# A two-block sequence kernel: the values' weighing in the forward state sweep, on VectorE or on GpSimd

## The chip, the cores and the metric

The kernel runs on one core of a Trainium2 chip. The metric is the device time of one execution in microseconds (us), as the median of several executions. The engines are named as in the profile: PE is TensorE's matmul, PEld its weight load, DVE is VectorE, ACT is ScalarE, POOL is GpSimd, SP is SyncE, which here only issues DMAs.

## The reference, cut to what matters

Two network blocks follow each other on 1024 tokens of width 1024 in float32. The second one has a bidirectional state-space mixer with 16 heads of 64 values, 2 groups and a state of 128. It works in chunks of 128 tokens. For one direction:

```python
xdt = (xs * dt[..., None]).reshape(b, nc, CHUNK, g, r, p)
acs = jnp.cumsum((dt * a).reshape(b, nc, CHUNK, g, r), axis=2)
decay = jnp.exp(jnp.where(lower, acs[:, :, :, None] - acs[:, :, None, :], -jnp.inf))
cb = jnp.einsum('bctgn,bcsgn->bctsg', cc, bc)
y_diag = jnp.einsum('bctsgr,bcsgrp->bctgrp', cb[..., None] * decay, xdt)
st = jnp.einsum('bcsgn,bcsgr,bcsgrp->bcgrpn', bc, jnp.exp(acs[:, :, -1:] - acs), xdt)
def step(s, inp):            # one chunk after the other
    dec, add = inp
    return s * dec[..., None, None] + add, s
y_off = jnp.einsum('bctgn,bcgrpn,bctgr->bctgrp', cc, s_in, jnp.exp(acs))
```

The product `st` takes the values (xs) of a chunk multiplied by one weight per token and head, dt * exp(acs_last - acs). This multiplication is the weighing that the change is about. It gives 128 tokens x 1024 values.

## The kernel before, in words

Everything but the scan is matrix products, for which a stream of 512 KB weight tiles is loaded by SP into `w_raw`. Each tile is split by GpSimd into a high and a low part, a cast at L195 and a subtraction at L197 (`stream_split`), and multiplied by TensorE at L204, L206 and L208. The scan of the second block is `phase5`, a block of its own: all engines meet at its end before the next phase (`phase6`) starts, whose first work is to load the rows that the scan left in memory (L2737 to L2739).

`phase5` has two halves. In the backward sweep (loop at L2642) the chunks are walked from the last to the first while TensorE also works on the stream's last sixteen tiles before the pool weights. GpSimd splits those and, last, the two tiles of the pool weights; it has no instruction in the forward half. The order of each engine's work is the order of its code; semaphores tie the engines together.

The forward sweep walks the eight chunks (i = 0 to 7). Each engine runs its own loop:

- VectorE (L2674): `add_decays(i)`, two sums of exponentials (L2664); `last_sum(i - 1)`, which ends the output rows of the chunk before (L2669, waits for TensorE's diagonal product) and, for the first five chunks, also makes the low part of a pooled tile (L2672, waits for ScalarE's high part L2579); two products of the decays with `cb` (L2681, `w_ready`, one for each group); the off-diagonal rows out of PSUM (L2688) and their addition (L2691); the state's update, times the decay (L2694) and plus the product in PSUM (L2695, `state_ready`); and the weighing of the next chunk's values into `xw` (`weigh(i + 1, 0)`, which is L2594, `xw_ready`). The weighing of chunk 0 stands ahead of the loop (L2659).
- TensorE (`forward`, L2469): the off-diagonal product (L2473, waits for `state_ready`); the state's product from `xw` (L2479, waits for `xw_ready` and for `y_ready`, which `last_sum(i - 1)` gives, and signals `st_done`); four exponent products of the next chunk (L2456, L2459, each waits for the exponential two before it); `cb` of the next chunk (L2465); the 16 diagonal products (L2489).
- ScalarE (L2571): four exponentials for the next chunk (L2558; the first two wait also for the `w_ready` of group 0 of the current chunk, the last two for that of group 1); a copy of `cb` (L2566); 16 copies that make the moving rows of the chunk after that (L2522); for i below 5 the high part (L2579).
- SP loads the backward sweep's output rows and the pooled tiles (L2394, L2398).

`xw` is one buffer. Its reader is the state's product L2479. L2594 is also the line of the weighings in the backward sweep and for the context, since they share the helper `weigh`.

Of the kernel before, what the change touches and what calls it, by code (L numbers as in the profile page):

```python
# [16 lines left out]
NC = SEQ // P  # L17
# [112 lines left out]
def bc(ap, dim, n):  # L130

    ap = ap.unsqueeze(dim)
    shape = list(ap.shape)
    shape[dim] = n
    return ap.broadcast_to(shape)
# [52 lines left out]
def stream_split(pool, k, first, last):  # L188

    for n in range(first, last):  # L190
        s = n % 2
        pool.wait_ge(k.w_loaded[s], (n // 2 + 1) * 16)
        if n >= 2:
            pool.wait_ge(k.tile_done, n - 1)
        pool.tensor_copy(k.w_hi[:, s, :], k.w_raw[:, s, :]).then_inc(k.w_high, 1)  # L195
        pool.wait_ge(k.w_high, n + 1)
        pool.tensor_tensor(k.w_lo[:, s, :], k.w_raw[:, s, :], k.w_hi[:, s, :].bitcast(F32),  # L197
                           ALU.subtract).then_inc(k.w_split, 1)
# [820 lines left out]
def signals(nc, ctx, stage, names):  # L1019

    return {n: ctx.enter_context(nc.semaphore(f"{stage}_{n}")) for n in names.split()}
# [1300 lines left out]
def phase5(nc, k, d, v):  # L2322
# [4 lines left out]
    with ExitStack() as ctx:  # L2327
        def sb(n, shape, dt=F32):
            return ctx.enter_context(nc.sbuf_tensor(n, shape, dt))

        def over(n, tile):
# [3 lines left out]
        state, y_even, xw = (sb(n, [P, SEQ]) for n in ("state5", "y5", "xw5"))  # L2335
# [21 lines left out]
        s = signals(nc, ctx, "p5", "chain xw_ready moving_ready d_done e_ready e_sum w_ready cb_done cb_ready off_done fore_ready fore_added "  # L2357
                                   "st_done state_ready diag_done y_ready y_back y_out0 y_out1 y_in0 y_in1 z_out d_out "
                                   "d_in dhi dlo x_done x_free0 x_free1 cleared area_in pooled")
# [10 lines left out]
        fwd = back + BWD_JOBS * NC  # L2370
        block = ctx.enter_context(nc.Block())

        def heads(ap):
            return ap.rearrange("p (h n) -> p h n", h=SSM_HEADS)

        def values(c):
            return heads(v.tok[:, c, VAL:VAL + D_MODEL])

        def per_head(buf, c, r, n=HDIM):

            return bc(buf[:, c, SSM_HEADS * r:SSM_HEADS * (r + 1)], 2, n)

        @block.sync
        def _(sp):
            stream_load(sp, k, XBC_END + 4, UZ_END + 4)
            sp.wait_ge(s["z_out"], 16 * KT)
            for i in range(NC):
                if i < 2:
                    sp.wait_ge(s["y_back"], 16 * NC)
                else:  # L2390
                    sp.wait_ge(y_out[i % 2], 16 * (i // 2))
                if i == 1:
                    sp.wait_ge(k.tile_done, UZ_END)
                sp.dma_start(y_of[i % 2], d.y_tok[i, :, :]).then_inc(y_in[i % 2], 16)  # L2394
                if i < SPLIT_EARLY:
                    sp.wait_ge(s["d_out"], 16 * KT)
                    sp.wait_ge(s["dlo"], i)
                    sp.dma_start(stage[:, :], d.u_scr[i, :, :]).then_inc(s["d_in"], 16)  # L2398

        @block.gpsimd  # L2400
        def _(pool):
            pool.memset(big[:, 0:2, :], 0.0).then_inc(s["cleared"], 1)
            pool.memset(pad[:, :], 0.0).then_inc(s["cleared"], 1)
            stream_split(pool, k, XBC_END + 2, UZ_END + 2)

        @block.tensor
        def _(pe):
# [180 lines left out]
        def _(dve):  # L2588
# [3 lines left out]
            def weigh(c, r, out=xw[:, :]):  # L2592

                tt(heads(out), values(c), per_head(v.w_st, c, r), ALU.mult).then_inc(s["xw_ready"], 1)  # L2594
# [61 lines left out]
            dve.wait_ge(s["pooled"], KT)  # L2656
            dve.wait_ge(x_free[1], fwd // 2)
            dve.tensor_copy(state[:, :].rearrange("p (a n) -> p a n", a=4), state_f).then_inc(s["state_ready"], 1)
            weigh(0, 0)  # L2659

            def add_decays(i):
                for g in range(NGRP):
                    dve.wait_ge(s["e_ready"], EXPS * i + 2 * g + 2)
                    tt(big[:, 2 * g, :], big[:, 2 * g, :], big[:, 2 * g + 1, :], ALU.add).then_inc(s["e_sum"], 1)  # L2664

            def last_sum(i):
                dve.wait_ge(s["diag_done"], i + 1)
                dve.wait_ge(s["fore_added"], i + 1)
                tt(y_of[i % 2], y_of[i % 2], Xf[(i + 1) % 2], ALU.add).then_inc(s["y_ready"], 1)  # L2669
                if i < SPLIT_EARLY:  # L2670
                    dve.wait_ge(s["dhi"], i + 1)
                    tt(v.a_lo[:, i, :], stage[:, :], v.a_hi[:, i, :].bitcast(F32), ALU.subtract).then_inc(s["dlo"], 1)  # L2672

            for i in range(NC):  # L2674
                add_decays(i)
                if i:
                    last_sum(i - 1)
                dve.wait_ge(s["cb_ready"], i + 1)
                for g in range(NGRP):
                    dve.wait_ge(s["e_sum"], 2 * i + g + 1)  # L2680
                    tt(weights[g].rearrange("p (h t) -> p h t", h=HPG), big[:, 2 * g, :].rearrange("p (h t) -> p h t", h=HPG),  # L2681
                       bc(cb[:, g, :], 1, HPG), ALU.mult).then_inc(s["w_ready"], 1)
                dve.wait_ge(s["off_done"], i + 1)
                if i:
                    dve.wait_ge(s["y_ready"], NC + i)
                else:
                    dve.wait_ge(s["d_out"], 16 * KT)
                tt(heads(fore_tmp), heads(Xf[(i + 1) % 2]), per_head(v.e_acs, i, 0), ALU.mult).then_inc(s["fore_ready"], 1)  # L2688
                dve.wait_ge(y_in[i % 2], 16 * (i // 2 + 1))
                dve.wait_ge(s["fore_ready"], i + 1)  # L2690
                tt(y_of[i % 2], y_of[i % 2], fore_tmp, ALU.add).then_inc(s["fore_added"], 1)  # L2691
                dve.wait_ge(s["st_done"], i + 1)
                dve.wait_ge(s["state_ready"], i + 1)
                ch.link(tt(heads(state[:, :]), heads(state[:, :]), per_head(v.e_tot, i, 0), ALU.mult))  # L2694
                tt(state[:, :], state[:, :], Xf[i % 2], ALU.add).then_inc(s["state_ready"], 1)  # L2695
                if i + 1 < NC:
                    weigh(i + 1, 0)
            last_sum(NC - 1)


# [241 lines left out]
def build(nc, arrays, out):  # L2942
# [14 lines left out]
    with ExitStack() as ctx:  # L2957
        k = open_kit(nc, ctx, d)
        phase1(nc, k, d)
        with ExitStack() as half:  # L2960
            w = open_work(nc, half, "b1", k)
            turn1 = Turn(nc, half, "n1", k, w, lambda t: k.vecs[:, VEC["mix_post"][0] + t:VEC["mix_post"][0] + t + 1],
                         (lambda t: k.vecs[:, VEC["mlp_pre"][0] + t:VEC["mlp_pre"][0] + t + 1], None), loads=True)
            turn2 = Turn(nc, half, "n2", k, w, lambda t: k.vecs[:, VEC["mlp_post"][0] + t:VEC["mlp_post"][0] + t + 1],
                         (lambda t: k.mod[:, MOD_AX, t:t + 1], lambda t: k.mod[:, MOD_BX, t:t + 1]))
            one_block(nc, phase2(nc, half, k, d, w, turn1),
                      mlp_phase(nc, half, k, d, w, P1_TILES + P2_TILES, "m1", turn1, turn2, ada=True,
                                out=d.x2_scr, ahead=True))
        with ExitStack() as half:
            clear_semaphores(nc)  # L2970
            v = open_scan(nc, half, k)
            phase4(nc, k, d, v)
            phase5(nc, k, d, v)
        with ExitStack() as half:
            clear_semaphores(nc)
            w = open_work(nc, half, "b2", k)
            turn3 = Turn(nc, half, "n3", k, w, lambda t: k.mod[:, MOD_G1, t:t + 1],
                         (lambda t: k.mod[:, MOD_A2, t:t + 1], lambda t: k.mod[:, MOD_B2, t:t + 1]), loads=True)
            turn4 = Turn(nc, half, "n4", k, w, lambda t: k.mod[:, MOD_G2, t:t + 1])
            one_block(nc, phase6(nc, half, k, d, w, turn3),  # L2980
                      mlp_phase(nc, half, k, d, w, OUT2_END, "m2", turn3, turn4, out=out))
# [146 lines left out]
```

## Time and profile before

| what | us |
|---|---|
| median of 3 runs | 2850.29 (2841.47 to 2863.74) |
| the profiled execution, its own time | 2847.84 |
| its span, first to last instruction | 2846.1 |
| PE busy | 2690.4 (95%) |
| DVE busy | 1659.4 (58%) |
| POOL busy | 987.9 (35%) |
| ACT busy | 607.8 (21%) |

The span is what the trace's clock covers; 1.74 us of the profiled execution's own time lie around it. All start times are counted from the span's start. In the timelines a row is one instruction, or several alike in a row (x2), with start, duration, engine, line, output <- inputs, and in brackets how long the engine had been idle and what ended that. PE is busy nearly throughout over the whole program, but shares of a whole program say little of one stage: the forward sweep is the stretch from 1740 to 1852 us.

### The profile page before, as it was taken

The numbers are of one execution on the slowest core, as the hardware profiler recorded it, in microseconds if no ns is written. First come the engines' busy times: TensorE is split into PE (matmuls) and PEld (weight loads), VectorE is DVE, ScalarE is ACT, GpSimd is POOL, SyncE is SP. The second block draws the span as 40 slices with busy tenths as digits, with TensorE's granted clock in tenths as the row PEclk, the third lists the DMA queues.
The fourth block names the chain that finished last, engine by engine and source line by source line (L and its number), as shares of the span: only waits on it lengthen the run. The fifth ranks groups of instructions, "written<-read, shape, count | busy, mean of one in ns | idle before, by whom it ended". The sixth has DMA issues, their size and how long they took to land. (4 is left out here: it accounts for less than half of the span.)

```text
span 2846.1 us, 32173 instructions
## 1 busy us (share of the span) xinstructions
PE 2690.4 (95%) x12390; PEld 2144.4 (75%) x12390; DVE 1659.4 (58%) x2219; ACT 607.8 (21%) x871; POOL 987.9 (35%) x515
## 2 busy tenths in 40 slices
PE   8889999999999999987898999989999999999997
PEld 5777877778888888766775776578767888888885
DVE  7887545756555665676747986953475222222247
ACT  4323232310110001133331104632131110001111
POOL 2212226553433333541212331023645333333353
PEclk9999999999999999998999999999999999999998
DMA  3111132223222232231001333241332111111122
GB/s 139 38 53 49 44 140 89 89 82 111 89 87 92 93 103 94 91 108 53 30 29 41 115 119 115 100 172 43 118 97 83 51 44 52 44 52 44 52 68 103
DMA packets 88484, 228.88 MB, mean 80 GB/s; under 512 B 27520, under 2 KB 30720, under 8 KB 88384
## 3 DMA queue, kind: packets, MB, share of 16 engines
q1 hardware_dynamic: 52384, 172.81, 18.5%
q10 hardware_dynamic: 36000, 54.69, 6.2%
q8 instruction: 68, 1.11, 0.2%
q14 instruction: 32, 0.26, 0.0%
HBM read 197.98 MB, written 28.31 MB: 80 GB/s over the span
## 5 line engine op out<-in xcount | busy, mean ns | idle before, releaser
L195 POOL CAST w_hi<-w_raw 128x1024 fp32r<-128x1024 f32 x254 | 288.3, 1135 | 1793.4 <-PE ps L208 1775.9
L204 PE MATMUL ps<-a_hi,w_hi 128*128 128x512 f32 x2080 | 693.3, 401 | 46.6 <-PEq L2931 14.6
L197 POOL TENSOR_TENSOR w_lo<-w_raw,w_hi 128x1024 fp32r<-128x1024 f32 x254 | 696.6, 2743 | 20.4
L206 PE MATMUL ps<-a_lo,w_hi 128*128 128x512 f32 x2080 | 677.8, 393 | 0.0
L208 PE MATMUL ps<-a_hi,w_lo 128*128 128x512 f32 x2080 | 675.2, 392 | 0.0
L204 PEld LDWEIGHTS ps<-a_hi,w_hi 128*128 128x128 f32 x2080 | 390.2, 190 | 148.9 <-issue 57.6
L206 PEld LDWEIGHTS ps<-a_lo,w_hi 128*128 128x128 f32 x2080 | 395.7, 190 | 83.4
L208 PEld LDWEIGHTS ps<-a_hi,w_lo 128*128 128x128 f32 x2080 | 394.7, 190 | 84.6
L206 PE MATMUL ps<-g_b,w_hi 128*128 128x512 f32 x1216 | 421.1, 397 | 0.0
L204 PE MATMUL ps<-g_b,w_hi 128*128 128x512 f32 x1088 | 369.4, 396 | 10.3 <-DVE g_b L1792 10.3
L208 PE MATMUL ps<-g_b,w_lo 128*128 128x512 f32 x1088 | 370.0, 397 | 0.0
L206 PEld LDWEIGHTS ps<-g_b,w_hi 128*128 128x128 f32 x1216 | 229.6, 189 | 53.4
L204 PEld LDWEIGHTS ps<-g_b,w_hi 128*128 128x128 f32 x1088 | 204.9, 188 | 67.6 <-DVE g_b L1792 14.2
L208 PEld LDWEIGHTS ps<-g_b,w_lo 128*128 128x128 f32 x1088 | 205.0, 188 | 49.9
L1750 ACT ACTIVATE tmp_b<-ps 128x1024 f32<-128x1024 f32 x48 | 49.3, 1027 | 863.6 <-PE ps L208 863.6
L1872 DVE TENSOR_TENSOR tmp_b<-tmp_b 128x1024 f32<-128x1024 f32 x48 | 58.8, 1225 | 299.1 <-ACT tmp_b L1750 299.1
L1885 DVE TENSOR_TENSOR mix_b<-mix_b,ps 128x1024 f32<-128x1024 f32 x48 | 58.6, 1220 | 250.6 <-PE ps L208 250.6
L1874 DVE TENSOR_TENSOR g_b<-tmp_b,g_b 128x1024 fp32r<-128x1024 f32 x48 | 106.6, 2220 | 54.1 <-ACT g_b L1754 54.1
L1144 DVE TENSOR_TENSOR acc_b<-acc_b,tmp_b 128x512 f32<-128x512 f32 x56 | 77.2, 1378 | 23.9 <-ACT tmp_b L1103 20.6
L2258 DVE SCALAR_TENSOR_TENSOR cv<-raw,vecs,cv 128x1284 f32<-128x1284 f32 (+1 forms) x48 | 80.4, 1676 | 5.3 <-DVE cv L2256 0.6
L1864 DVE SCALAR_TENSOR_TENSOR ada_sum_m<-ada_w,c_silu,ada_sum_m 128x128 f32<-128x128 f32 x252 | 74.7, 346 | 3.0
L1864 DVE SCALAR_TENSOR_TENSOR ada_sum_m<-ada_w_m,c_silu,ada_sum_m 128x128 f32<-128x128 f32 x252 | 74.6, 344 | 3.0
(459 smaller groups left out, 2680.6 us busy)
## 6 DMA issues: line engine op xcount, KB each, us to landing
w_raw<-in_wstream SPq DMA_DIRECT2D x254, 512.0 KB, 3.4
ada_w<-in_ada_w ACTq DMA_DIRECT2D x25, 512.0 KB, 3.5
ada_w_m<-in_ada_w ACTq DMA_DIRECT2D x25, 512.0 KB, 3.4
y_by_token<-y ACTq DMA_DIRECT2D x12, 512.0 KB, 3.3
x_res_b<-in_xT SPq DMA_DIRECT2D x2, 2048.0 KB, 11.5
x_block<-x_res_b SPq DMA_DIRECT2D x16, 256.0 KB, 3.1
z_rows<-ada_w ACTq DMA_DIRECT2D x8, 512.0 KB, 2.9
u_rows<-pad ACTq DMA_DIRECT2D x8, 512.0 KB, 4.2
```

The source lines that it names most:

```text
L195: pool.tensor_copy(k.w_hi[:, s, :], k.w_raw[:, s, :]).then_inc(k.w_high, 1)
L197: pool.tensor_tensor(k.w_lo[:, s, :], k.w_raw[:, s, :], k.w_hi[:, s, :].bitcast(F32), ALU.subtract).then_inc(k.w_split, 1)
L204: pe.matmul(o, w_hi, a_hi[:, c], start=first, stop=False)
L206: pe.matmul(o, w_hi, a_lo[:, c], start=False, stop=False)
L208: ins = pe.matmul(o, w_lo, a_hi[:, c], start=False, stop=last)
L1144: dve.tensor_tensor(w.acc[:, cols], w.acc[:, cols], w.tmp[:, t % 2, cols], ALU.add).then_inc(self.added, 1)
L1750: act.activation(w.tmp[:, t % 2, :], pair[t % 2], ACT.Relu).then_inc(k.pair_free[t % 2], 1)
L1864: ins = dve.scalar_tensor_tensor(out=sums, in0=weights, scalar=k.c_silu[:, kt, c:c + 1], in1=sums, op0=ALU.mult, op1=ALU.add)
L1872: tt(w.tmp[:, t % 2, :], w.tmp[:, t % 2, :], w.tmp[:, t % 2, :], ALU.mult).then_inc(s["square"], 1)
L1874: tt(w.g_lo[:, t, :], w.tmp[:, t % 2, :], w.g_hi[:, t, :].bitcast(F32), ALU.subtract)\
L1885: tt(w.mix[:, 2 * t, :], w.mix[:, 2 * t, :], pair[q], ALU.add).then_inc(k.pair_free[q], 1)
L2258: ins = stt(out=out, in0=raw[:, m:m + cols], scalar=tap(m), in1=out, op0=ALU.mult, op1=ALU.add)
```

## The change

GpSimd, once it has split its last tile, makes the weighed values of all eight chunks. The weighing of chunk 0 waits for the last product of the backward sweep, that of chunk i for the state's product of chunk i - 1, because both use the one `xw`. VectorE no longer weighs in the forward sweep. Nothing else changes, and `xw_ready` counts as before.

```diff
@@ gpsimd of phase5 @@
             stream_split(pool, k, XBC_END + 2, UZ_END + 2)
+            pool.wait_ge(s["x_done"], fwd)
+            for i in range(NC):
+                if i:
+                    pool.wait_ge(s["st_done"], i)
+                pool.tensor_tensor(heads(xw[:, :]), values(i), per_head(v.w_st, i, 0), ALU.mult).then_inc(s["xw_ready"], 1)
@@ vector of phase5 @@
             dve.tensor_copy(state[:, :].rearrange("p (a n) -> p a n", a=4), state_f).then_inc(s["state_ready"], 1)
-            weigh(0, 0)
@@ the loop's end @@
                 tt(state[:, :], state[:, :], Xf[i % 2], ALU.add).then_inc(s["state_ready"], 1)
-                if i + 1 < NC:
-                    weigh(i + 1, 0)
             last_sum(NC - 1)
```

## Rows read from the trace of the kernel before

**Rows 1.** Busy time in two stretches of the sweep.

```profile
core 0: us, PE busy (x) PEld busy (x) DVE busy (x) ACT busy (x) POOL busy (x), PEclk, DMA share, GB/s
1740.00:1756.00 16.00, 13.41 (x40) 6.03 (x40) 9.96 (x9) 12.86 (x25) 2.97 (x2) 1.00 0.50 171
1756.00:1830.00 74.00, 71.44 (x344) 44.50 (x344) 66.50 (x58) 55.94 (x127) 0.00 (x0) 1.00 0.28 100
```

**Rows 2.** The chain that ended last, just after the sweep: start, length.

```profile
1860.01 26.97 DMA mix_b<-z_rows
```

**Rows 3.** Timeline of VectorE in the forward sweep: an early period, and starts of later ones.

```profile
1761.65 1.22 DVE L2669 TENSOR_TENSOR y<-y,ps 128x1024 f32<-128x1024 f32 x1 [1.88 <-PE ps L2489]
1764.43 1.22 DVE L2672 TENSOR_TENSOR a_lo<-ada_w,a_hi 128x1024 fp32r<-128x1024 f32 x1 [1.55 <-ACT a_hi L2579]
1765.57 2.35 DVE L2681 TENSOR_TENSOR tok<-big,pad 128x1024 f32<-128x1024 f32 x2
...
1772.70 1.22 DVE L2594 TENSOR_TENSOR xw<-tok,w_st 128x1024 f32<-128x1024 f32 x1
1773.83 2.35 DVE L2664 TENSOR_TENSOR big<-big 128x1024 f32<-128x1024 f32 x2
1776.10 1.22 DVE L2669 TENSOR_TENSOR y_odd<-y_odd,ps 128x1024 f32<-128x1024 f32 x1
1777.65 1.22 DVE L2672 TENSOR_TENSOR a_lo<-ada_w,a_hi 128x1024 fp32r<-128x1024 f32 x1 [0.33 <-ACT a_hi L2579]
...
1818.56 1.23 DVE L2672 TENSOR_TENSOR a_lo<-ada_w,a_hi 128x1024 fp32r<-128x1024 f32 x1 [0.94 <-ACT a_hi L2579]
...
1830.23 1.21 DVE L2669 TENSOR_TENSOR y_odd<-y_odd,ps 128x1024 f32<-128x1024 f32 x1
...
1842.86 1.22 DVE L2669 TENSOR_TENSOR y<-y,ps 128x1024 f32<-128x1024 f32 x1 [0.88 <-PE ps L2489]
```

**Rows 4.** Timeline of ScalarE: the first exponential of three chunks.

```profile
1766.88 1.94 ACT L2558 ACTIVATE big<-ps 128x1024 f32<-128x1024 f32 x2 [2.49 <-DVE tok L2681]
...
1780.59 1.03 ACT L2558 ACTIVATE big<-ps 128x1024 f32<-128x1024 f32 x1 [2.97 <-PE ps L2459]
...
1834.71 1.03 ACT L2558 ACTIVATE big<-ps 128x1024 f32<-128x1024 f32 x1 [3.88 <-PE ps L2459]
```

**Rows 5.** Timeline of TensorE: a tile's last product, and the state's product twice.

```profile
1738.81 0.61 PE L208 MATMUL ps<-a_hi,w_lo 128*128 128x512 f32 x2
...
1748.23 1.88 PE L2479 MATMUL ps<-xw,tok 128*128 128x512 f32 x4
...
1763.23 1.88 PE L2479 MATMUL ps<-xw,tok 128*128 128x512 f32 x4
```

**Rows 6.** Timeline, GpSimd in the backward sweep, and its last split.

```profile
1655.16 3.38 POOL L197 TENSOR_TENSOR w_lo<-w_raw,w_hi 128x1024 fp32r<-128x1024 f32 x1
1663.91 1.69 POOL L195 CAST w_hi<-w_raw 128x1024 fp32r<-128x1024 f32 x1 [5.37 <-PE ps L208]
1665.67 3.24 POOL L197 TENSOR_TENSOR w_lo<-w_raw,w_hi 128x1024 fp32r<-128x1024 f32 x1
...
1739.57 1.04 POOL L195 CAST w_hi<-w_raw 128x1024 fp32r<-128x1024 f32 x1 [6.44 <-PE ps L208]
1740.68 2.37 POOL L197 TENSOR_TENSOR w_lo<-w_raw,w_hi 128x1024 fp32r<-128x1024 f32 x1
```

**Rows 7.** Timeline of VectorE beside those splits.

```profile
1654.10 2.19 DVE L2624 TENSOR_TENSOR tok<-big 128x1152 f32<-128x1152 f32 x1
1656.33 3.30 DVE L2624 TENSOR_TENSOR pad<-tok 128x1024 f32<-128x1024 f32 x1
...
1663.47 1.22 DVE L2631 TENSOR_TENSOR pad<-pad,big 128x1024 f32<-128x1024 f32 x1
1664.62 2.06 DVE L2645 TENSOR_TENSOR y<-tok,head_rows 128x1024 f32<-128x1024 f32 x1
1666.71 1.22 DVE L2647 TENSOR_TENSOR big<-ps,e_acs 128x1024 f32<-128x1024 f32 x1
```

## The prediction

> **What bounds the kernel now.** First I read the page: PE is busy for 95% of the span, so a stage counts only where PE waits in it. Then the busy time by stretch [rows 1]: from 1756 to 1830 VectorE is busy 66.50 of 74 us and PE 71.44, but PE's number holds waits between short groups of matmuls, and GpSimd does nothing at all. So the forward sweep is a loop over several engines, which has to be read from the timelines. Third, the chain of waits behind the sweep: the load of the scan's rows, 26.97 us long, is issued at 1860.01, once the scan's block has ended, and the chain that ended last runs through it [rows 2]. A microsecond more or less in the sweep is therefore one in the whole time.
>
> Then the timelines of one early period, engine by engine. Name four starts per chunk: Y, the output sum L2669; A, the low part L2672; E, the first exponential L2558; S, the end of the state's product L2479. The reader is to see that few distances tie them together:
>
> - A to the next Y by VectorE's own work: 1764.43 to 1776.10, 11.67 us, no wait between [rows 3]. It holds the two L2681, L2688, L2691, L2694, L2695, the weighing L2594 and two L2664.
> - A to E over the decay product of group 0: 1764.43 to 1766.88, 2.45 [rows 3, 4]; ScalarE had waited 2.49 for L2681.
> - Y to E over TensorE (state's product, then the exponents): 1776.10 to 1780.59, 4.49, where ScalarE waited for the PE [rows 3, 4].
> - E to the A that follows, over ScalarE (four exponentials, the copy of cb, 16 moving rows, the high part): 1766.88 to 1777.65, 10.77 [rows 3, 4].
> - E to the next Y over exponentials, cb and diagonal products: 1834.71 to 1842.86, 8.15 [rows 3, 4].
>
> The five early periods (chunks with a low part, A at 1764.43 up to 1818.56) take 54.13 / 4 = 13.53 each. ScalarE's ring A-E-A alone is 2.45 + 10.77 = 13.22; VectorE's ring is 11.67 plus the 1.14 from Y to A, 12.81 without a wait. So ScalarE's ring bounds the early periods, and VectorE waits 0.33 to 1.55 before L2672 for the high part. Y to Y over TensorE is 4.48 + 8.15 = 12.63, which is what the late period 1830.23 to 1842.86 takes; VectorE waits 0.88 there [rows 3].
>
> **The change, part by part.** Removed from VectorE: the weighing, from its start to the next start 1773.83 - 1772.70 = 1.13 us, seven times in the loop [rows 3]. The eighth, ahead of the loop, lies in a wait. A to Y becomes 11.67 - 1.13 = 10.54. If that were all, Y would be bound by E + 8.15 = A + 10.60, and a period would be ScalarE's 13.22. The fifth A would stand at 1764.43 + 4 x 13.22 = 1817.31, its E at 1819.76, the next Y at 1827.91 instead of 1830.23: 2.32 us gained, not 7 x 1.13 = 7.9, because ScalarE and TensorE are late next.
>
> Added on GpSimd: eight products of 128x1024 with two inputs. None is in the trace. The nearest row is the subtraction L197 of the same size on the same engine, 2.37 us with VectorE quiet [rows 6]. The ends are the one-input cast, 1.04 [rows 6], and twice the subtraction, 4.74, for the input that repeats one weight over 64 values; on VectorE the same form costs no more than a plain one (L2594 beside L2672, both 1.22) [rows 3]. I take 2.37.
>
> Is it hidden from TensorE? Chunk 0: GpSimd's split ends at 1740.68 + 2.37 = 1743.05 [rows 6], the product at 1745.4; the state's product of chunk 0 starts at 1748.23 [rows 5]. Chunk i: starts at S, ends 2.4 later (4.8 at the upper end), and is wanted a period later. So the new wait costs TensorE nothing. The waits on GpSimd hold up nothing either: behind them is only the end of the block, as its next split needs a tile of the next phase. No DMA is moved.
>
> What isn't hidden is VectorE. Where GpSimd and VectorE both work out of SBUF, the backward sweep shows them taking turns [rows 6, 7]. The L197 at 1655.16 lasts 3.38, since it stands behind an L2624 that ends at 1656.29; the next L2624, issued at 1656.33, lasts 3.30 and ends 1.09 after GpSimd is done. The same width takes 1.22 alone: a loss of 2.08. L2645, issued at 1664.62 while the cast waits since 1663.91, loses 0.84 (2.06 for 1.22): the waiting GpSimd instruction gets in even between two VectorE instructions that follow each other without a wait (1.15 from start to start). L2647, one of whose inputs is in PSUM, runs its 1.22 in the middle of an L197 [rows 7]. So a VectorE instruction with both inputs in SBUF loses 2.08 when GpSimd's product is ahead of it, one that reads PSUM loses nothing.
>
> The Trainium skill ("SBUF — State Buffer", section on who interferes with whom) says that the shared ports are an exclusive lock held for a whole instruction, taken also by a VectorE instruction with two SBUF inputs against a GpSimd one that reads SBUF. The rows above agree. By its "fully blocks" each collision would cost the whole 2.37 instead of 2.08, which would make the result below 1.5 us later (five times 0.29).
>
> Where does it meet VectorE? S is 1763.23 + 1.88 = 1765.11, which is Y + 3.46 [rows 3, 5]. GpSimd starts 0.15 after the PE ends (an estimate: the last cast starts at 1739.57, its tile's last product ends at 1738.81 + 0.61 = 1739.42, rows 5, 6). That is 1765.26, in the middle of L2672 (1764.43 to 1765.65). Behind this stands the decay product L2681 of group 0, both inputs in SBUF, and on it hangs E. So A to E becomes 2.45 + 2.08 = 4.53, right in the bounding ring, and A to Y 10.54 + 2.08 = 12.62. Then E = 1764.43 + 4.53 = 1768.96, Y = E + 8.15 = 1777.11, A = E + 10.77 = 1779.73. A is 2.62 after Y, GpSimd comes at Y + 3.61, 0.99 into L2672, which ends at 1.22: the same collision again, and so for all five low parts. A period is 4.53 + 10.77 = 15.30. The fifth A is at 1764.43 + 4 x 15.30 = 1825.63, E at 1830.16, Y at 1838.31, against 1830.23: 8.1 us later.
>
> The other three weighings cost nothing. That of chunk 0 meets L2664 in a stretch where VectorE waits for exponentials. That of chunk 1 delays L2691, but the Y at 1761.65 had waited 1.88 for the PE. In the late period without a low part, GpSimd comes as the second L2681 ends and delays only L2691 and the state, by about 1 us; VectorE's ring is then 10.54 + 1 = 11.5 at most, and TensorE's 12.63 bounds, as before.
>
> Sum: -2.3 (VectorE's work removed, what of it shows) and +10.4 (5 x 2.08) = +8.1 us. On the profiled execution's own 2847.84 that is 2855.9; I say 2856. The median of the three runs shown is 2.45 above the profiled execution, so beside it the same sum gives 2858.4, inside the range.
>
> **The rivals.**
>
> 1. *VectorE isn't held up.* If VectorE's next instruction kept its turn in front of a waiting GpSimd, or the new product didn't clash, only the gain is left: -2.3, 2845.5, faster than before. For it: VectorE's pairs here follow at 1.14, the closest the trace has. Against: L2645 lost 0.84 in that position [rows 7]. It decides if L2681 of group 0 keeps its 1.2 us while GpSimd waits.
> 2. *GpSimd comes later than L2672's end*, which lacks only 0.2 to 0.4 us. Then group 0 of L2681 goes first, and group 1 is held, which only the third exponential needs. The loop settles otherwise: A to Y is 12.62, A comes 1.4 after Y, E follows from Y over TensorE at A + 3.1, a period is 3.1 + 10.9 = 14.0. The fifth A is at 1764.43 + 4 x 14.0 = 1820.4, the next Y at 1833.1: +2.8, 2850.7. For it: the small margin, and GpSimd's start after a semaphore is my estimate. Against: the first collision starts from rows that the change doesn't touch.
> 3. *The product is slower on GpSimd than the subtraction*, because of the repeated weight. Each us more is paid five times; at 4.74 it is 5 x 2.37 = 11.9 more, +20, 2867.8. For it: no broadcast operand on GpSimd is in the trace. Against: nothing in the rows makes one cost more. With the cast's 1.04 it would be 5 x 1.33 less, +1.4, 2849.3.
>
> **How the numbers follow.** Forecast 0.50, rival 1 0.13, rival 2 0.17, rival 3 0.20, mostly in milder form. The range runs from rival 1 to rival 3, 2845 to 2869, and so takes in the ends of the unknown product. The forecast's own range is 2852 to 2862, for the scatter of single runs and the 2.45 between median and profile. A measurement of this kernel can tell about 1%, 28.5 us, from no change; every case lies within it: within 1% 0.94, slower 0.04 (a product above three times the subtraction, or more collisions), faster 0.02.
>
> **What would show it.** L2594 is gone from the forward sweep, and eight GpSimd products of about 2.4 us, 3.3 with the wait in front, stand there. In five of them the L2681 of group 0 lasts 3.3 instead of 1.2, and ScalarE waits some 4.5 for it. The five early low parts stand 15.3 apart, and the block's end is 8 us later. The state's product never waits for `xw`. The granted clock in the sweep is 1.00 before [rows 1]; if the longer waits of the PE lowered it, that would be a cost I haven't counted. Wrong would be: low parts 13.2 apart (rival 1), 14.0 with long second L2681 (rival 2), GpSimd products of 4 us and more (rival 3).

## The result, and the profile after

Over 20 runs of each kernel the change takes 2868.07 us (2858.34 to 2879.59) against 2849.55 (2837.95 to 2864.84): 18.5 us more (17.2 between the means), ratio 1.006 with a 95% interval of [1.004, 1.008]. That is slower, and by less than 1%. The direction was forecast, the size was not: 8.1 us. The profiled execution is further off still, 2877.12 against 2847.84.

The first lines to read are the timelines of VectorE and GpSimd. The lines of TensorE and ScalarE are 5 higher than before (L2484 was L2479, L2494 was L2489, L2563 was L2558), those of VectorE's loop 4 (L2673 was L2669, L2676 was L2672, L2685 was L2681, L2695 was L2691). VectorE after the change, two periods that answer to [rows 3]:

```profile
1789.13 1.22 DVE L2673 TENSOR_TENSOR y_odd<-y_odd,ps 128x1024 f32<-128x1024 f32 x1 [1.57 <-PE ps L2494]
1791.91 1.23 DVE L2676 TENSOR_TENSOR a_lo<-ada_w,a_hi 128x1024 fp32r<-128x1024 f32 x1 [1.55 <-ACT a_hi L2584]
1793.05 4.06 DVE L2685 TENSOR_TENSOR tok<-big,pad 128x1024 f32<-128x1024 f32 x2
...
1808.62 1.22 DVE L2673 TENSOR_TENSOR y<-y,ps 128x1024 f32<-128x1024 f32 x1 [4.38 <-PE ps L2494]
1809.75 1.22 DVE L2676 TENSOR_TENSOR a_lo<-ada_w,a_hi 128x1024 fp32r<-128x1024 f32 x1
1810.89 2.35 DVE L2685 TENSOR_TENSOR tok<-big,pad 128x1024 f32<-128x1024 f32 x2
1813.16 1.21 DVE L2692 TENSOR_TENSOR pad<-ps,e_acs 128x1024 f32<-128x1024 f32 x1
1814.48 2.57 DVE L2695 TENSOR_TENSOR y_odd<-y_odd,pad 128x1024 f32<-128x1024 f32 x1
...
1826.07 1.23 DVE L2676 TENSOR_TENSOR a_lo<-ada_w,a_hi 128x1024 fp32r<-128x1024 f32 x1 [1.55 <-ACT a_hi L2584]
```

GpSimd after the change, in the same periods:

```profile
1792.67 2.23 POOL L2409 TENSOR_TENSOR xw<-tok,w_st 128x1024 f32<-128x1024 f32 x1 [10.84 <-PE ps L2484]
1814.07 1.91 POOL L2409 TENSOR_TENSOR xw<-tok,w_st 128x1024 f32<-128x1024 f32 x1 [19.17 <-PE ps L2484]
```

At 1792.67 GpSimd comes 0.76 into the low part L2676, as forecast, and the pair of L2685 takes 4.06 instead of 2.35: the collision, at 1.71 us. But the next output sum waits 4.38 for the PE, the next low part follows at once, and there the product comes too late for L2685 and meets L2695. The low parts at 1791.91 and 1826.07 are two periods apart, 34.16 us, 17.08 each, where I forecast 15.30 and [rows 3] had 13.53. TensorE's own timeline, after the change, says why:

```profile
1794.31 0.73 PE L2464 MATMUL ps<-moving,l_rows 64*128 64x512 f32 x2
1797.15 0.74 PE L2461 MATMUL ps<-scan_square 128*128 128x512 f32 x2 [2.10 <-ACT big L2563]
1797.81 0.74 PE L2464 MATMUL ps<-moving,l_rows 64*128 64x512 f32 x2
1798.48 1.08 PE L2461 MATMUL ps<-scan_square 128*128 128x512 f32 x2
1799.49 1.22 PE L2464 MATMUL ps<-moving,l_rows 64*128 64x512 f32 x2
1800.64 1.22 PE L2470 MATMUL ps<-bcT 128*128 128x128 f32 x4
1801.65 6.93 PE L2494 MATMUL ps<-tok 128*128 128x64 f32 x32
```

The PE waits 2.10 us. From 1.3 us after it has gone on, the same pairs of matmuls take longer, first 1.08 and then 1.22 instead of 0.73, and the 32 diagonal matmuls take 6.93 instead of 3.68. That is TensorE's clock going from 2.4 to 1.2 GHz. The busy times by stretch after the change, with the granted clock in the column before the last two, show three such stretches where [rows 1] had 1.00:

```profile
1756.00:1778.00 22.00, 20.54 (x57) 13.26 (x58) 11.08 (x10) 11.50 (x27) 1.76 (x1) 0.54 0.09 33
1778.00:1798.00 20.00, 17.90 (x75) 10.11 (x75) 16.74 (x12) 11.91 (x24) 4.12 (x2) 1.00 0.37 130
1798.00:1812.00 14.00, 14.00 (x47) 10.27 (x47) 9.48 (x9) 8.05 (x21) 0.00 (x0) 0.52 0.09 37
1812.00:1832.00 20.00, 17.90 (x76) 10.11 (x74) 16.73 (x13) 11.75 (x24) 4.13 (x2) 0.99 0.38 132
1832.00:1846.00 14.00, 14.00 (x47) 10.33 (x47) 9.47 (x9) 8.21 (x21) 0.00 (x0) 0.53 0.08 34
```

The second and third follow a wait of 2.1 us each. The first, in the period of chunk 0, follows a wait of 1.98 us that the kernel before has too. So two things were open: whether the collision or the new wait on `xw` costs, and whether the falls of the clock belong to the change.

I measure the sweep by itself from here on: from the copy of the state (L2658 before) to the start of the last output sum (L2669). Before it is 1736.77 to 1851.37, 114.60 us; after, 1742.14 to 1879.91, 137.77.

### The profile page after: what moved, and what is told of

The parts are those of the page before. It is cut to its first block and busy times, and to the rows that moved or that the text cites. A ratio compares the mean times of both kernels' runs of the same rounds, so it can differ in the third digit from the quotient of the medians.

```text
span 2875.3 us, 32173 instructions
## 1 busy us (share of the span) xinstructions
PE 2720.0 (95%) x12390; PEld 2165.2 (75%) x12390; DVE 1658.1 (58%) x2211; ACT 608.1 (21%) x871; POOL 1002.2 (35%) x523
```

## The experiments

**The change, once more.**

> The change itself, once more. Theory (clock): the excess over the 8.1 us of the forecast comes from TensorE's granted clock, which falls to half after a collision has made the PE wait 2.1 us; then the profile shows again two or three stretches of the sweep with the diagonal products L2494 at about 6.9 us for 32 instead of 3.7, and the time is 15 to 20 us above the kernel before. Rival (chance): the slow stretches of the one profile were an accident of that execution; then this profile shows other ones or none, and a sweep about 8 us longer than before.

2873.8 us (12 runs), ratio 1.0054 [1.003, 1.0078]. The sweep takes 137.80; the PE again waits 2.10 twice, at the same places, and L2494 takes 6.93 three times. The pattern is not an accident of one execution. The difference of the medians is only 14.0 us this time, that of the means 17.1: the times of the kernel before lie in two groups, so its median jumps by 10 us (2859.79 beside this run) and its mean by 4.

**The kernel before, a second look.**

> The kernel before, unchanged, for a second profile. Its times lie in two groups, about 2838 to 2853 and 2857 to 2867. Theory: the upper group are executions in which the clock falls once in the sweep, in the period of chunk 0, after the PE's wait of about 2 us for the moving rows; a profile of the upper group shows L2489 of chunk 0 at 6.9 us, one of the lower group 3.7 throughout. Rival: the groups come from another stage, and the sweep is the same in both.

This execution took 2860.46, the upper group. The PE before, second look:

```profile
1757.87 1.02 PE L2456 MATMUL ps<-scan_square 128*128 128x512 f32 x2 [1.97 <-ACT moving L2522]
1767.88 6.93 PE L2489 MATMUL ps<-tok 128*128 128x64 f32 x32
...
1785.81 3.68 PE L2489 MATMUL ps<-tok 128*128 128x64 f32 x32
```

So the kernel before has the fall of chunk 0 too, in this execution, after the same wait of 1.97 for the moving rows. Its sweep is then 1742.55 to 1866.64, 124.09: 9.5 us more than 114.60. The sweep also starts 5.8 us later than in the first profile; in the window from 1530 to 1600 the clock is 0.91 there, where it was 1.00. Every profile of this study with about 0.9 in that window also has the fall of chunk 0, if the wait is left in. Why the two go together stays open. For comparing sweeps it means that like must go with like: 124.09 is what stands beside the 137.77 of the change. The difference is 13.7, not 23.2.

The end of the sweep differs between the two profiles of the kernel before as well. The PE, first profile and second look:

```profile
1847.54 3.79 PE L2489 MATMUL ps<-tok 128*128 128x64 f32 x32 [1.23 <-DVE pad L2688]
```

```profile
1861.61 5.00 PE L2489 MATMUL ps<-tok 128*128 128x64 f32 x32 [1.23 <-DVE pad L2688]
```

Behind this wait of 1.23 the last diagonal products take 3.79 in eight of the study's twelve profiles, and 5.00 to 5.55 in four: this one, both of the change, and one kernel further below. So 1.2 of the 9.5 us belong to the end, and the fall of chunk 0 alone is worth 8.3. Measured only to the last output sum but one, which stands ahead of that wait, the sweep is 106.09 in the first profile (1736.77 to 1842.86) and 114.38 in this one (1742.55 to 1856.93). Where two sweeps differ at their end I compare these shorter times.

**The product a little later.** GpSimd also waits for the decay products:

```diff
                 if i:
                     pool.wait_ge(s["st_done"], i)
+                    pool.wait_ge(s["w_ready"], 2 * i)
```

> GpSimd waits also for both decay products of the chunk before (w_ready), so it starts behind VectorE's second L2685, beside L2692, which reads PSUM. Theory (collision): no L2685 is lengthened any more, the PE doesn't wait 2.1 us for the exponentials, only L2695 is delayed by 0.5 to 1.3 us; the clock stays up in the sweep and the time is that of the kernel before or up to 3 us less. Rival (any GpSimd product costs): the time stays within 5 us of the change's, 15 to 20 above before.

2845.18 us, ratio 0.997 [0.9944, 0.9996] against the kernel before. The collision has moved; VectorE of this kernel (L2686 is the decay product, L2696 the addition):

```profile
1816.44 1.23 DVE L2677 TENSOR_TENSOR a_lo<-ada_w,a_hi 128x1024 fp32r<-128x1024 f32 x1 [0.95 <-ACT a_hi L2585]
1817.58 2.35 DVE L2686 TENSOR_TENSOR tok<-big,pad 128x1024 f32<-128x1024 f32 x2
1819.85 1.22 DVE L2693 TENSOR_TENSOR pad<-ps,e_acs 128x1024 f32<-128x1024 f32 x1
1821.17 1.89 DVE L2696 TENSOR_TENSOR y<-y,pad 128x1024 f32<-128x1024 f32 x1
1822.99 1.21 DVE L2699 TENSOR_TENSOR state<-state,e_tot 128x1024 f32<-128x1024 f32 x1
```

VectorE loses 0.66 (1.89 for 1.23) at a place where it then still waits 0.8 to 0.95 for the high part. The later periods are 13.23 to 13.36, and no fall follows a decay product. This execution has the fall of chunk 0; its sweep of 121.94 stands beside 124.09, 2.15 us less. But its last diagonal products take 3.79, so 1.2 of that is the end. To the last output sum but one it is 113.44 beside 114.38: 0.9 us less. The same kernel was run again:

> late_weigh once more, for a firmer ratio. Theory: VectorE's relief without a collision is worth the 2.2 us seen in the sweep, the ratio to before is 0.998 to 0.9995. Rival: the 0.997 was scatter of the two groups of times, and this one is 1.000 or above.

Ratio 0.9999 [0.9976, 1.0022], the sweep again 121.94. The sweep's gain of 0.9 repeats (the 2.2 of the expectation took the sweep's end for a part of it), and the total doesn't show it: 1 us lies below what the two groups of times let a dozen runs tell. The one line takes away all of the change's cost; that it beats the kernel before is not shown.

**Only one weighing.** The seven others are left out of the computation, so VectorE is relieved and nothing collides:

```diff
-            for i in range(NC):
-                if i:
-                    pool.wait_ge(s["st_done"], i)
-                pool.tensor_tensor(heads(xw[:, :]), values(i), ...)
+            pool.tensor_tensor(heads(xw[:, :]), values(0), ...)
...
-                pe.wait_ge(s["xw_ready"], back + NC + i + 1)
+                pe.wait_ge(s["xw_ready"], back + NC + 1)
```

> Only chunk 0 is weighed, by GpSimd; the state's products of the other chunks read the same xw, so seven weighings are left out of the computation. Theory: what the removal from VectorE alone is worth, by the rings of the forecast 2.3 us less than before, with early low parts 13.2 apart, and no fall of the clock beyond those of the kernel before. Rival (VectorE bounds): 7 x 1.13 = 7.9 us less. Rival (the clock falls from VectorE's being early, not from collisions): 10 us or more above before.

2854.31 us, ratio 0.9982 [0.9958, 1.0005]. The low parts stand 13.24 apart (1791.78, 1805.02, 1818.25, 1831.48), and each had waited 1.5 us for ScalarE's high part: VectorE isn't the bound. The sweep with the fall of chunk 0 is 121.19, 2.9 less than 124.09, but this one too has 3.79 at its end. To the last output sum but one it is 112.69 beside 114.38: 1.7 us less. The forecast had 2.3, the rival 7.9.

**GpSimd's product, and VectorE keeps its own.** (The diff leaves out the lines that declare the buffer and the semaphore.)

```diff
+            for i in range(1, NC):
+                pool.wait_ge(s["st_done"], i)
+                if i > 1:
+                    pool.wait_ge(s["extra"], i - 1)
+                pool.tensor_tensor(heads(extra[:, :]), values(i), per_head(v.w_st, i, 0), ALU.mult).then_inc(s["extra"], 1)
```

> The kernel before, whose VectorE weighs as it did; GpSimd makes seven products of the same form at the same moments (after st_done) into a buffer that nobody reads. Theory (collision): with the low part standing 1.55 to 2.2 after the output sum, GpSimd comes at the end of the first or in the second decay product, and once a decay product of group 0 is held by about 1.7 us the PE waits and the clock falls, so the time is 8 to 20 us above before. Rival (the change's wait on xw costs, not the collision): no more than 1 us above before.

2872.27 us, ratio 1.0058 [1.0035, 1.0081]. Nobody waits for these products, and the cost is that of the change. The place was expected wrongly: the product comes 0.76 into the first low part, since that one stands 2.78 after its output sum, as in [rows 3]. VectorE and GpSimd of this kernel (L2687 is the decay product):

```profile
1768.54 1.23 DVE L2678 TENSOR_TENSOR a_lo<-ada_w,a_hi 128x1024 fp32r<-128x1024 f32 x1 [1.55 <-ACT a_hi L2585]
1769.68 4.06 DVE L2687 TENSOR_TENSOR tok<-big,pad 128x1024 f32<-128x1024 f32 x2
```

```profile
1769.30 2.23 POOL L2410 TENSOR_TENSOR extra<-tok,w_st 128x1024 f32<-128x1024 f32 x1 [12.81 <-PE ps L2485]
```

No fall in chunk 0 here, but three behind the three collisions (stretches at 0.61, 0.66 and 0.66), each after a PE wait of 2.1. The sweep is 136.87, 22.3 more than 114.60.

**VectorE delayed without GpSimd.** The kernel before, with an addition in front of the decay products, five times (its buffer's declaration is left out of the diff):

```diff
                     tt(v.a_lo[:, i, :], stage[:, :], v.a_hi[:, i, :].bitcast(F32), ALU.subtract).then_inc(s["dlo"], 1)
+                    ch.link(tt(extra[:, :, :], v.tok[:, 0:2, VAL:VAL + 768], v.tok[:, 2:4, VAL:VAL + 768], ALU.add))
```

> The kernel before, GpSimd idle in the sweep; VectorE gets one more addition (1536 columns, about 1.8 us, result unused) between the low part and the decay products, five times. Theory (any delay of the decay product makes the PE wait, and the wait brings the clock down): the PE waits about 2 us for the exponentials, the clock falls two or three times, 12 to 25 us above before. Rival (only the sharing of SBUF costs): VectorE's and ScalarE's rings add 1.8 us in five periods at most, no fall of the clock, 5 to 9 us above before.

2870.31 us, ratio 1.0067 [1.0039, 1.0095]; the sweep is 137.04. VectorE (L2683 is the decay product), and the PE, of this kernel:

```profile
1768.54 1.75 DVE L2674 TENSOR_TENSOR extra<-tok 128x1536 f32<-128x1536 f32 x1
1770.33 2.36 DVE L2683 TENSOR_TENSOR tok<-big,pad 128x1024 f32<-128x1024 f32 x2
```

```profile
1772.72 1.22 PE L2457 MATMUL ps<-scan_square 128*128 128x512 f32 x2 [2.19 <-ACT big L2559]
1773.87 1.22 PE L2460 MATMUL ps<-moving,l_rows 64*128 64x512 f32 x2
```

A delay of 1.8 us by an ordinary instruction gives the same PE wait, the same falls (three) and the same time as a collision of 1.7. The sharing of SBUF matters only by the delay it makes.

**More work for the PE.** The change, with matmuls repeated where the PE would wait:

```diff
+                    for _ in range(2 if g == 0 and 2 <= i <= SPLIT_EARLY + 1 else 1):
                         for out in outs:
                             pe.matmul(out, ident_r, bc(masks[r], 1, HPG // 2), start=True, stop=False)
...
                     ins.then_inc(s["d_done"], 1)
```

> The change, with more work for the PE: the first two exponent products of chunks 2 to 6 are made twice (the second time over the first), 2.6 us of matmuls each, before ScalarE may read them. They lie in the PE's wait for the decay product. Theory (the wait lowers the clock): with five collisions of 1.71 and the clock up, the sweep is only 5 to 9 us longer than before, so more work makes the kernel 5 to 12 us faster than the change. Rival (the clock falls for another reason, or the fall costs little): the time is that of the change or above it.

2859.27 us, ratio to the kernel before 1.0027 [1.0, 1.0053]: 8.8 us below the change's median of 2868.07. The ratios, 1.0027 and 1.006, are the better comparison, since each stands on runs of the kernel before made beside it; their intervals overlap, so the totals alone leave the gain likely and not shown. In the profile all five low parts now collide, with the clock at 1.00 through the sweep. This is the second fastest of the 12 executions (2852.03; the slowest took 2873.19), so whether the clock stays up in every one isn't known. VectorE of this kernel:

```profile
1766.10 1.23 DVE L2678 TENSOR_TENSOR a_lo<-ada_w,a_hi 128x1024 fp32r<-128x1024 f32 x1 [1.55 <-ACT a_hi L2586]
1767.24 4.06 DVE L2687 TENSOR_TENSOR tok<-big,pad 128x1024 f32<-128x1024 f32 x2
...
1778.75 1.22 DVE L2675 TENSOR_TENSOR y_odd<-y_odd,ps 128x1024 f32<-128x1024 f32 x1 [0.32 <-PE ps L2496]
1781.53 1.23 DVE L2678 TENSOR_TENSOR a_lo<-ada_w,a_hi 128x1024 fp32r<-128x1024 f32 x1 [1.56 <-ACT a_hi L2586]
1782.67 4.06 DVE L2687 TENSOR_TENSOR tok<-big,pad 128x1024 f32<-128x1024 f32 x2
```

The periods are 15.42 (1766.10, 1781.53, 1796.95, 1812.36, 1827.79), the sweep 123.26, 8.7 us more than 114.60 with the same end. That is close to the forecast of 15.30 and 8.1, but in part by luck. The collision costs 1.71 where I forecast 2.08, which makes a period of 13.22 + 1.71 = 14.93. The rest is the filler's own price: the second exponential now waits for a repeated product, where in the kernel before it followed the first at once. ScalarE before, and of this kernel:

```profile
1793.95 1.03 ACT L2558 ACTIVATE big<-ps 128x1024 f32<-128x1024 f32 x1 [2.49 <-DVE tok L2681]
1795.13 1.02 ACT L2558 ACTIVATE big<-ps 128x1024 f32<-128x1024 f32 x1
```

```profile
1785.69 1.03 ACT L2565 ACTIVATE big<-ps 128x1024 f32<-128x1024 f32 x1 [4.20 <-DVE tok L2687]
1787.35 1.02 ACT L2565 ACTIVATE big<-ps 128x1024 f32<-128x1024 f32 x1 [0.63 <-PE ps L2465]
```

From start to start it is 1.66 instead of 1.18, 0.48 us at each of the five collisions.

**Filling the wait of chunk 0**, in the late kernel and in the kernel before:

```diff
-                for g in range(NGRP):
+                for g in [g for _ in range(1 if i else 2) for g in range(NGRP)]:
                     ins = pe.matmul(X[st_at][:, g, :], v.tok[:, i, g * P:(g + 1) * P], xw[:, half_of(g)], ...)
```

> late_weigh, and the state's product of chunk 0 is made twice, so that the PE's wait of 2.0 us for the moving rows of chunk 1 is cut to below 0.5. Theory: the fall of the clock in the period of chunk 0 is gone from all executions, the upper group of times vanishes or thins, and the median is at or below late_weigh's lower group, 2842 to 2846. Rival (that fall has another cause): two groups as in late_weigh, median the same.

> The kernel before, with the state's product of chunk 0 made twice so that the PE waits 0.3 instead of 2.0 us for the moving rows of chunk 1. Theory: the fall of the clock in the period of chunk 0, worth 9.5 us of sweep, is gone from every execution; the sweep from the state's copy to the last output sum is 114 to 116 us and the upper group, 2857 to 2867, moves down by 5 to 10 us. Rival (the clock falls later instead): the sweep is 118 or more, and the times stay where they are.

In the late kernel the fall of chunk 0 is gone (the PE waits 0.25, the diagonal products take 3.68), and nothing is above 2857.22. But the times fill the middle, median 2851.45, ratio 0.9991 [0.997, 1.0013]; the profiled one has a fall at the sweep's end, where the last diagonal products take 5.55 behind the wait of 1.23. The expected median of 2842 to 2846 was missed. The late kernel's sweep to the last output sum but one is 104.69, 1.4 less than the 106.11 of the kernel before with the same filling, both without the fall of chunk 0. In the kernel before it came as expected: sweep 114.61, although the clock was 0.83 from 1520 to 1560, no run above 2853.65 where 8 of the 23 runs beside it were above 2860, median 2847.89, ratio 0.9975 [0.9951, 0.9999]. The PE of this kernel:

```profile
1755.68 0.73 PE L2456 MATMUL ps<-scan_square 128*128 128x512 f32 x2 [0.26 <-ACT moving L2522]
1761.53 3.68 PE L2489 MATMUL ps<-tok 128*128 128x64 f32 x32
```

Of all kernels run, this one and the late one were below the kernel before by their intervals, once each, and for the late one the second measurement didn't confirm it.

## Why the prediction was right or wrong

**The removal gains 2.3 us, not 7.9: right in its mechanism, 1.7 where it could be measured.** With one weighing, and beside the kernel before with the same fall in chunk 0, the four early periods take 56.06 instead of 56.63 and the way from the fifth low part to the next output sum 10.54 instead of 11.68. The forecast had 1.25 and 1.07 for these two. The first is smaller because the first of the four periods, still under the fallen clock, takes 16.3 in both. No profile has this kernel without that fall. ScalarE's ring of 13.22 bounds the early periods, measured 13.24.

**GpSimd's product takes 2.37: too much.** It takes 1.90 us with nothing in its way (2.23 behind a low part). The broadcast operand didn't make it dearer. The bounds held, and rival 3 fell.

**A collision costs 2.08: a fifth too much.** It is 1.71 (4.06 for 2.35), beside a product that is 0.47 shorter than the one I took. Place and order were right: GpSimd starts 3.54 after the output sum (forecast 3.61), in the middle of the low part, and goes in front of the decay product. That GpSimd gets in between two VectorE instructions 1.14 apart, which rival 1 doubted, is seen in every collision.

**The other weighings, the wait on `xw` and the late period cost nothing: right in the sum.** The state's product never waits for `xw`.

**Five collisions in a row, 15.30 each, 8.1 in all: only while TensorE's clock stays up, and then too much.** The filler shows the five in a row, and its 15.42 and 8.7 agree with the numbers by luck: the sum with the measured collision is -2.3 + 5 x 1.71 = 6.2 us (an estimate; no run shows it without the filler), and the filler's own 5 x 0.48 = 2.4 us makes up the rest. The step that failed is the sum's silent one: that TensorE's matmuls keep their durations. The text named a lower clock as a cost that it had not counted; it should have had a price. A collision makes the PE wait 2.1 us where it waited 0.4 or not at all ahead of these products, and the clock falls behind it. The diagonal products then take 6.93, and the period with the fall is 17.84 (1791.91 to 1809.75). The fall in turn delays the next state's product so that its collision misses the decay product; that period is 16.32. So the five collisions become two, with two falls, or three with three where chunk 0 has none. It comes to 13.7 us of sweep beside the kernel before with its own fall (137.77 - 124.09). For executions without a fall in chunk 0 there is no profile of the change; the two kernels with the same delays were 22.3 and 22.4 longer. The measured 18.5 lies between. That isn't a full account: eight of the change's 20 executions took 2858 to 2864, some 15 us above the lower group of the kernel before, where 22 would be expected, and which falls they have isn't known.

**The rivals.** Rival 1, VectorE not held up, fell: 4.06 for the pair. Rival 2, GpSimd later than the low part, occurs, but as a consequence of the fallen clock, in every second period. None of my rivals was the one that counted, and the forecast's own range, 2852 to 2862, missed the median of 2868.07; the wide one, to 2869, held it only because of a rival that was wrong, and by 0.9 us; the second measurement's median, 2873.8, lies outside it. That is luck, not a forecast of this cost.

The Trainium skill ("TensorE: Matmul & The Clock Gate", section on HAM oscillation) says that gaps in the PE's work can throttle its clock and that the work behind a gap then runs cold. The traces agree for the waits behind a collision: 2.4 GHz before the wait of 2.10, 1.2 GHz from 1.3 us after it. The wait of 2.0 in chunk 0 was followed by a fall in six of the ten profiles that have it, so a gap alone doesn't decide.

## What to carry to other kernels

When work is moved from VectorE to GpSimd, ask which VectorE instruction stands next when GpSimd starts, and whether it has both inputs in SBUF; one added wait that puts the start beside an instruction that reads PSUM took away the whole cost here. A delay on the ring that feeds TensorE has two prices, the delay and the clock that the wait brings down: here the second added at least 5 us to the sweep (13.7 against 8.7 with the clock held, the filler's own price included). Compare profiles only with the same falls of the clock, or the one you happened to catch explains more than the edit does.

## What the runs showed of the hardware that was not expected

- A wait of 2.0 to 2.2 us of an otherwise busy PE was followed by a fall from 2.4 to 1.2 GHz in all seven cases behind a held decay product in the change's two profiles and in the kernel with the extra product, and in three more with the delayed VectorE; waits of 0.2 to 0.9 us inside the sweep never were. The wait of 1.97 in chunk 0 was followed by one in six of ten profiles, the wait of 1.23 at the sweep's end in four of twelve. The fall of chunk 0 (8.3 us) goes with the upper of the two groups of times of the kernel before, some 16 us apart; with that wait filled the upper group was gone.
- GpSimd's float32 product of 128x1024 with an operand repeated over 64 values took 1.90 us, its subtraction of two full operands 2.37. Whether the repeated operand, the operation or the output type makes the difference wasn't tried.
- More matmuls can make a kernel faster: five times 2.6 us of repeated products took the change's sweep from 137.77 to 123.26 in the profiled executions, and 1.7 us more in chunk 0 of the kernel before gave a ratio of 0.9975 [0.9951, 0.9999], measured once.
